# A mixture of 32 experts on one core: both halves of the rows in one stationary, half of w1 multiplied in fp32, and finished rows added into the output by DMA

## What is computed

```python
order = jnp.argsort(flat_e)               # 1024 routed rows, by expert
xb = x_pad[slot_tok].reshape(nb, MOE_BLOCK, D)
hid = jax.nn.silu(xblk @ w1[e]) * (xblk @ w3[e])   # w1, w3: 1024 x 512
yb = hid @ w2[e]                                   # w2: 512 x 1024
y = zeros.at[slot_tok].add(yb * slot_w[:, None])   # weight of the row
x = x + y
```

## Time and profile before

| | before |
|---|---|
| median of 3 runs | 1926.95 us (1926.22 to 1927.83) |
| the profiled execution, its own time | 1926.94 us |
| its span | 1925.1 us |
| TensorE busy | 1723.3 us, 90% |
| VectorE, ScalarE, GpSimd busy | 1145.4, 895.0, 797.3 us |
| bytes moved | 357.94 MB |

### The profile page before, as it was taken

The page is one execution under the profiler, slowest core; times in us unless marked ns, Lnnn a source line. Parts: engine busy times, 40 slices in busy tenths (PEclk is TensorE's granted clock), DMA queues, the critical chain, the costliest instruction groups (busy, mean ns, idle before and its releaser), DMA issues.

```text
span 1925.1 us, 22731 instructions
## 1 busy us (share of the span) xinstructions
PE 1723.3 (90%) x7364; PEld 1250.4 (65%) x7364; DVE 1145.4 (59%) x1523; ACT 895.0 (46%) x1196; POOL 797.3 (41%) x388
## 2 busy tenths in 40 slices
PE   2899999899998989989689997964999999999992
PEld 2788888687785867468577476752666665666661
DVE  5677773725133464334754224225889999999984
ACT  3554443432323220123431034332888888888882
POOL 0688883333341442114101031201566656665562
PEclk9899999999998999989769998976999999999997
DMA  8343443222331434132004322123999999999995
GB/s 284 99 132 110 120 165 125 94 87 73 132 113 65 170 127 161 58 127 88 1 1 129 112 107 88 44 88 104 360 386 397 395 390 390 393 397 394 388 360 186
DMA packets 138669, 357.94 MB, mean 186 GB/s; under 512 B 12661, under 2 KB 64125, under 8 KB 113768
## 3 DMA queue, kind: packets, MB, share of 16 engines
q1 hardware_dynamic: 130050, 324.88, 46.0%
q10 hardware_dynamic: 4758, 19.31, 2.6%
q0 software_dynamic: 3792, 12.85, 2.1%
HBM read 333.95 MB, written 23.07 MB: 185 GB/s over the span
## 4 chain that ended last, share of the span: by engine, by line
PE 54%; issue 17%; POOL 12%; DVE 11%; DMA 2%; ACT 2%; POOLq 0%; DVEq 0%; SPq 0%; ACTq 0%
PE ps L694 13%; PE ps L696 13%; PE ps L695 13%; PE ps L666 10%; POOL parts L2269 9%; PE ps L676 2%; POOL idx L2279 2%; DVE arena L1522 2%; PE ps L899 1%; PE ps L872 1%; DMA arena<-in_x 1%; POOL arena L2282 1%; DVE act_parts L1647 1%; DMA arena<-y_rows,dest_i 1%; DMA ring<-in_w_conv_out 1%
## 5 line engine op out<-in xcount | busy, mean ns | idle before, releaser
L2235 POOL TENSOR_TENSOR parts<-ring,parts 128x1024 fp32r<-128x1024 f32 x150 | 372.9, 2492 | 794.4 <-ACT parts L1058 791.4
L1351 ACT CAST parts<-ring 128x1024 fp32r<-128x1024 f32 x384 | 396.1, 1048 | 90.9 <-PE ps L696 66.9
L694 PE MATMUL ps<-parts,act_parts 128*128 128x512 f32 (+2 forms) x1088 | 427.8, 393 | 7.1 <-DVE parts L2059 2.2
L696 PE MATMUL ps<-parts,act_parts 128*128 128x512 f32 (+2 forms) x1088 | 423.9, 390 | 0.0
L695 PE MATMUL ps<-parts,act_parts 128*128 128x512 f32 (+2 forms) x1088 | 423.8, 390 | 0.0
L2059 DVE TENSOR_TENSOR parts<-ring,parts 128x1024 fp32r<-128x1024 f32 x289 | 394.1, 1415 | 26.4 <-ACT parts L1351 19.8
L2269 POOL TENSOR_TENSOR parts<-ring,parts 128x1024 fp32r<-128x1024 f32 x95 | 264.0, 2779 | 235.7 <-ACT parts L1351 235.0
L1058 ACT CAST parts<-ring 128x1024 fp32r<-128x1024 f32 x150 | 155.6, 1047 | 387.3 <-PE ps L696 297.3
L694 PE MATMUL ps<-act_parts,parts 128*128 128x512 f32 x640 | 253.0, 395 | 10.8 <-DVEq L1649 6.4
L695 PE MATMUL ps<-act_parts,parts 128*128 128x512 f32 x640 | 250.9, 392 | 0.0
L696 PE MATMUL ps<-act_parts,parts 128*128 128x512 f32 x640 | 250.7, 392 | 0.0
(11 more groups left out here) (248 smaller groups left out, 1837.9 us busy)
## 6 DMA issues: line engine op xcount, KB each, us to landing
ring<-in_w SPq DMA_DIRECT2D x192, 1024.0 KB, 7.2
ring<-in_w_in SPq DMA_DIRECT2D x30, 1024.0 KB, 7.2
ring<-in_w_in SPq DMA_DIRECT2D x34, 512.0 KB, 5.1
ring<-in_w_ada SPq DMA_DIRECT2D x12, 1024.0 KB, 14.5
ring<-in_w_ret_out SPq DMA_DIRECT2D x8, 1024.0 KB, 7.3
ring<-in_w_out SPq DMA_DIRECT2D x8, 1024.0 KB, 10.2
y_rows<-arena ACTq DMA_DIRECT2D x32, 256.0 KB, 6.3
ring<-in_w_in SPq DMA_DIRECT2D x16, 256.0 KB, 4.0
```

The lines of the kernel that those rows point to most:

```text
L694: pe.matmul(o, lhs[1], rhs[0], start=start, stop=False)
L696: return pe.matmul(o, lhs[0], rhs[0], start=False, stop=stop)
L1351: act.copy(parts[:, n % 4, 0, :], ring[:, j, n % 4 * 1024:(n % 4 + 1) * 1024]).then_inc(piece_hi, 1)
L2235: pool.tensor_tensor(parts[:, g % 4, 1, :], ring[:, st.place(j), k * 1024:(k + 1) * 1024], parts[:, g % 4, 0, :].bitcast(F32), ALU.subtrac ...
```

## The change

- **One stationary.** High and low rows of x stand side by side (`xgT` is now t, h, n). A piece of w1 or w3 is multiplied with 128 columns by its high half, then by its low half: two matmuls for three. The lower 64 rows of banks 1 and 2 then hold what the low rows gave, which ScalarE copies out (`low_up`) and VectorE adds in (`add_low`), before the sigmoid and the product.
- **w1's first half whole.** Pieces 0 and 1 are not split: four fp32 matmuls read them from the ring, against fp32 rows in `xg_whole` (64 columns of rows, 64 of zeros). Ten pieces a block are left to split (`PER_BLOCK`). The first half of w1 is free when TensorE has used it, and is loaded behind the second.
- **Rows added by DMA.** x is stored to `out` before the loop. The finished rows of a block, weighted already (`slot_w`, a fifth product in routing), are added into `out` by an indirect DMA from GpSimd's queue (`add_to_out`), which each turn waits for at its end (`added`). `y_rows`, its clearing, the store from ScalarE and all after the loop are gone.
- **Empty slots skipped.** An empty slot's index is 2048 or more, and gather and add leave it out (`bounds_check`).

```diff
-    ("h3T", KT, 1), ("route", from_bank(1, 4), 1), ("moe0", (0,), 1), ("moe_first", 4, 1),
+    ("h3T", KT, 1), ("route", from_bank(1, 5), 1), ("moe0", (0,), 1), ("moe_first", 4, 1),
...
+WHOLE = 2
+PER_BLOCK = 12 - WHOLE
...
@@ SyncE
-                for n in range(2):
+                for n in (0, 1) if j else (1, 0):
...
+            sp.dma_start(out_v, x).then_inc(out_done, 16)
...
@@ TensorE, up
-                    o = bank(stage, 1 + j, i)[0:SLOTS, :]
-                    for n in range(4):
+                    o = bank(stage, 1 + j, i)
+                    whole = 0 if j else WHOLE
+                    if whole:
+                        pe.wait_ge(xg_whole_ready, b + 1)
+                        pe.wait_ge(half_landed[0], (b + 1) * 16)
+                    for n in range(whole):
+                        for t in (2 * n, 2 * n + 1):
+                            mm = pe.matmul(o, xg_whole[:, t].rearrange("p h s -> p (h s)"), ring[:, 0, t * 512:(t + 1) * 512],
+                                           start=t == 0, stop=False)
+                        mm.then_inc(piece_split[n], 1)
+                    for n in range(whole, 4):
...
-                            mm = split_product(o, hi_lo(xgT[:, :, t, :]), hi_lo(parts[:, n, :, c * 512:(c + 1) * 512]),
-                                               t == 0, t == KT - 1)
+                            rows = xgT[:, t].rearrange("p h s -> p (h s)")
+                            pe.matmul(o, rows, parts[:, n, 0, c * 512:(c + 1) * 512], start=t == 0, stop=False)
+                            mm = pe.matmul(o, rows, parts[:, n, 1, c * 512:(c + 1) * 512], start=False, stop=t == KT - 1)
...
@@ ScalarE
             def high_rows(stage, k, i=0):
-                act.copy(xgT[:, 0].rearrange("p t n -> p (t n)"), full(stage, k, i)).then_inc(xgT_hi, 1)
+                o = full(stage, k, i).rearrange("p (t n) -> p t n", t=KT)
+                act.copy(xg_whole[:, :, 0, :], o[:, 0:2 * WHOLE, :]).then_inc(xg_whole_ready, 1)
+                act.copy(xgT[:, :, 0, :], o).then_inc(xgT_hi, 1)
...
+            def low_up(stage, j, i=0):
+                act.copy(up_low[j][0:SLOTS, :], full(stage, 1 + j, i)[SLOTS:2 * SLOTS, :]).then_inc(up_low_ready[j], 1)
+            def gate(stage, b, i=0):
+                act.wait_ge(up_sum_ready, b + 1)
+                act.activation(sg_h[0:SLOTS, :], full(stage, 1, i)[0:SLOTS, :], ACT.Sigmoid).then_inc(sg_h_ready, 1)
...
@@ VectorE
-            for n in range(3):
-                low(n, n)
+            low(2, 0)
...
+            own(dve.memset(xg_whole, 0.0))
+            for c in range(2 * MT):
+                own(dve.tensor_scalar(block_w[:, c, :], cst("iota"), blkf[:, c:c + 1], w01[:, c:c + 1], ALU.is_equal, ALU.mult))
...
             def add_rows(c):
-                dve.wait_ge(y_stored, (c + 1) * 16)
+                dve.wait_ge(y_blk_free, c + 1)
...
+            def add_low(stage, j, b, i=0):
+                dve.wait_ge(up_low_ready[j], b + 1)
+                o = full(stage, 1 + j, i)[0:SLOTS, :]
+                moe(dve.tensor_tensor(o, o, up_low[j][0:SLOTS, :], ALU.add))
...
@@ GpSimd
+            def add_to_out(c):
+                pool.wait_ge(y_sum_ready, c + 1)
+                pool.tensor_copy(idx_out[:, :], slot_tok[:, bass.ds(c, 1)]).then_inc(idx_out_ready, 1)
+                pool.wait_ge(idx_out_ready, c + 1)
+                pool.nop().then_inc(settled, 1)
+                pool.indirect_dma_start(out[0], bass.IndirectOffsetOnAxis(ap=idx_out[:, 0:1], axis=0), y_blk[0:SLOTS, :], None,
+                                        bounds_check=S - 1, oob_is_err=False, compute_op=ALU.add).then_inc(y_added, 16)
+            def added(c):
+                pool.wait_ge(y_added, (c + 1) * 16)
+                pool.nop().then_inc(y_blk_free, 1)
...
+            with pool.Fori(0, pool.snap(steps - 1)) as r:
+                turned("moe", r + 1)
+                gather(r + 3)
+                low(3, done + 3 - WHOLE)
+                add_to_out(r)
+                for n in (7, 11):
+                    low(n, done + n - WHOLE)
+                added(r)
```

More of the change, by code:

```diff
@@ L168 @@
 ]
[L169 removed]
+WHOLE = 2
+MOE_PIECES = [("moe_first", [n % 4 for n in range(WHOLE, 8)], 1), ("moe", [n % 4 for n in range(WHOLE, 12)], 1)]
+PER_BLOCK = 12 - WHOLE
 def mix_use(n, k):
@@ L368, in build @@
         taken[0] = expert_free + KT * S
-        combo = carve([4, D])
         y_low = carve([D])
+        up_low = [carve([FF]) for _ in range(2)]
+        xg_whole = carve([2 * WHOLE, 2, SLOTS])
+        block_w = carve([2 * MT, 64])
+        slot_w = carve([64])
         assert taken[0] <= MT * D + 10 * D + 2 * XD + D
@@ L975, in turn_slots @@
                 filled(stage, k, mm)
+            pe.wait_ge(block_w_ready, 1)
+            filled("route", 4, product(bank("route", 4)[0:SLOTS, 0:64], [slot_oh[:, q, :] for q in range(2 * MT)],
+                                       [block_w[:, q, :] for q in range(2 * MT)]))
             pe.wait_ge(plan_ready, 2)
@@ L1354, in _ @@
                 piece_released(act, g)
-            for n in range(4):
+            for n in range(WHOLE, 4):
                 high(n, 0)
@@ L1384, in low_rows @@
                              full("moe", 4 + g, c)[SLOTS:2 * SLOTS, :]).then_inc(y_low_ready, 1)
-            def store_rows(c):
-                act.wait_ge(y_sum_ready, c + 1)
-                act.dma_start(y_rows[bass.ds(c * SLOTS, SLOTS), :], y_blk[0:SLOTS, :]).then_inc(y_stored, 16)
             def down(c):
-                for n in range(3):
-                    high(8 + n, c, used=pieces["moe"].before(8 + n, c))
+                for n in range(8, 11):
+                    high(n, c, used=pieces["moe"].before(n - WHOLE, c))
+                    if n == 8:
+                        gate("moe", c + 1, c)
+                low_up("moe", 1, c)
                 high(11, c, ends=("moe", 2, c))
@@ L2127, in _ @@
             dve.nop().then_inc(plan_ready, 1)
-            own(dve.tensor_copy(slot_tok[:, :], full("route", 3)[0:SLOTS, 0:64]))
+            o = full("route", 3)[0:SLOTS, 0:64]
+            own(dve.tensor_scalar(slot_tok[:, :], o, float(SKIPPED), None, ALU.add))
+            own.wait()
+            own(dve.tensor_scalar(slot_tok[0:1, :], slot_tok[0:1, :], SKIPPED - 1, None, ALU.bitwise_and))
             own.wait()
```

160 lines of the change are left out of this document (76 added, 84 removed).

## The result

The changed kernel takes **1987.63 us** (median of 5 runs, 1978.89 to 1990.63) against 1926.95 of the kernel before: a ratio of 1.031, 95% interval 1.0285 to 1.0333. Slower, where 1896 us was forecast. The profiled run is the shortest of the five. One of the experiments further down, split_all_no_lower, had two disturbed executions of nine, the profiled one among them, so its time is the median of the other seven and it has no turn.

A forecast was written before the change was run, and what follows sets the result against it. Bound: a TensorE, ScalarE and GpSimd ring through one buffer, DMA engines nearly full beside it. Savings 20.7 + 1.8 + 3.9 + 5.1 = 31.5; 1925.1 - 31.5 + 1.8 = 1895.4, said as 1896 us; 8 in 10: 1884 to 1912.

The forecast's parts named there:

- Low 11 meets VectorE at PSUM work alone: 2.45: Loop, chain over GpSimd: its low half of piece 11 takes 2.45 us (2.39 to 2.76), ending at 17.1.
- chain of mine: Loop: two chains, over GpSimd (17.1 us) and over ScalarE (16.9), the longer counting; turn taken as 17.2, 5.1 saved.
- a sigmoid that waits: Loop, chain over ScalarE: the sigmoid also waits for VectorE's sum, up to 0.3 us more.
- The weighing of exclusion: Loop, piece 7's low half: the rule could cost 1.2 us (time 1914); rows show half, so 2.9 us taken.
- The bound is a ring of TensorE, ScalarE and GpSimd: Loop before the change: a closed chain through the one buffer of pieces 3, 7 and 11 sets the 17.37 us turn.
- The end: After the last sum of rows: index copy, one indirect DMA and its landing replace 27.7 us; 20.7 us saved.
- Start and blocks before the loop: Routing: 1.8 us saved; two `up`s outside the loop, each 1.96 us shorter: 3.9 us saved.
- The fp32 matmuls: In each `up`, four fp32 matmuls at 0.89 us each, 3.56 us together.
- The slower rival: Loop: GpSimd waits for the add's landing; from 10.7 us slower than before, at 14.5 the time 2045; chance 0.07.
- The 2.5 us more: Loop, each add: the rule on GpSimd writing descriptors would cost some 2.5 us more; the rows showed nothing of it.
- The ring or the DMA engines come out longer: Rival, loop: index checks, piece 7's low half or two stores cost more; turn 17.6 to 17.9, 1908 to 1917 us; chance 0.20.

The follow-up runs named there:

- split_all_no_lower: Changed kernel with pieces 0 and 1 split again, lower rows neither copied nor added, sigmoid and gate in their old places; 1930.34 us.
- gate_first: Changed kernel with one order changed: VectorE's gate stands ahead of the low half of piece 8; 1917.85 us.
- low11_on_vector: Changed kernel with the low half of piece 11 made by VectorE, GpSimd making only those of pieces 3 and 7; 1926.82 us.
- add_late: Changed kernel with the add issued between GpSimd's low halves of pieces 7 and 11, its landing waited for in the next turn; 1952.64 us.
- gate_first_low11_vector: gate_first with the low half of piece 11 made by VectorE; 1908.90 us.
- five_buffers: Changed kernel with a fifth buffer for split pieces, pieces 4 and 5 split ahead of the rows of the block before; 1998.71 us.

## Why the prediction was wrong, step by step

Cut into parts by the medians: the DMA part -17.9 us, products and lower rows with the gate ahead of low 8 +8.8, the gate behind low 8 +69.8.

- **The step that failed: "Low 11 meets VectorE at PSUM work alone: 2.45".** It came at low 10's start instead, and the price is not on low 11, which takes 2.46, but on low 10, which no chain of mine contained. 30 turns of 19.76 for 17.2 are 77 of the 84 us by which the profiled span is above the forecast one. VectorE came first in four of those 30 turns, and these are shorter (18.2 to 18.4 us from one first fp32 matmul of TensorE to the next, the others 19.1 to 20.9), but not 17.2. With low 10 never held, in gate_first, the turn is 17.64, 0.4 above the forecast. Why the gate matters: low 8 can't start before low 7 ends, whatever is ahead of it, so work on PSUM ahead of low 8 is hidden and behind it comes on top. I had the edit in the text only as a sigmoid that waits, on ScalarE's side. The section on the change doesn't show it either: VectorE's queue was gate, low 8, 9, 10 and became low 8, gate, low 9, 10.
- **The weighing of exclusion went the wrong way.** I set GpSimd's 3.04 us against the Trainium skill's rule in "SBUF — State Buffer", section "Who interferes with whom", took 0.65 for half an exclusion and went by it. The exclusion is whole, and 0.65 is what was left of VectorE's low 6 when low 7 began. The kernel before shows it on the *other* engine, in rows that I hadn't laid beside GpSimd's:
```profile
1507.62 3.50 DVE L2059 TENSOR_TENSOR parts<-ring,parts 128x1024 fp32r<-128x1024 f32 x3 [0.42 <-ACT parts L1351]
1511.03 0.68 DVE L2161 TENSOR_TENSOR arena<-ps,arena 64x512 f32<-64x512 f32 x1
1511.93 4.80 DVE L2059 TENSOR_TENSOR parts<-ring,parts 128x1024 fp32r<-128x1024 f32 x3 [0.22 <-DVE arena L2161]
```
  Low 7 (1510.34 to 1513.38) starts 0.77 us ahead of low 6's end and takes 0.7 longer than alone. Low 8, 9 and 10 take 4.80 us in place of 3.50, for low 8 waits until low 7 is over. With the Trainium skill's rule the traces agree in every overlapping pair of low halves: in all 19 traces, from 1330 us on, VectorE's record, where it ends last, does so by 1.08 to 1.16 us, and GpSimd's by 2.21 or more. They agree with the rule's other half too, that an operation with one SBUF input is not held: in gate_first 114 gates and adds from PSUM lie wholly inside a low half of GpSimd and take 0.67 to 0.68 us.
- **"The bound is a ring of TensorE, ScalarE and GpSimd"** left out that low halves cover 0.98 of the time before: 9 of VectorE at a pitch of 1.14 and 3 of GpSimd at 2.36 make 17.3 of 17.37 us. TensorE is as full, so which of the two binds is not shown. But taking 2 us from TensorE gave nothing: gate_first's turn is 17.64.
- **The end** was right in kind: 19.2 saved, not 20.7. The copy starts 0.4 behind the sum, not 0.1, and from the DMA's start to the end are 7.0 us, not 5.8. Not in the sum at all were the 2.6 us by which the stretch from the last low 11 to the last sum grew.
- **Start and blocks before the loop:** 3.3 saved, not 5.7. There too low 11 takes 3.27 us.
- **The fp32 matmuls** cost less than the 0.89 each that was forecast where the clock is up: in gate_first and low11_on_vector the next product starts 3.13 to 3.14 us behind the first of four in nearly every turn, not 3.56. In the changed kernel's loop it is 3.13 to 4.02, the longer where they begin at the lower clock.
- **The add** lands 7.8 us after its issue (median of 17 between 1450 and 1800), and 5.6% of the 16 engines' time is spent in its queue and the gather's. The slower rival needed 10.7 and didn't happen. GpSimd takes 1.5 us for it where the gather takes 1.0 to 1.4 (in add_late the add takes 2.4). The 2.5 us more that the prediction estimated from the Trainium skill's "SBUF — State Buffer", section "SBUF: two separate sides", were not seen in any turn.
- **"The ring or the DMA engines come out longer"**, 17.6 to 17.9 us, is the turn that gate_first shows: 17.64. I had no rival for a worse order.

**Left open:** why the turn doesn't fall under 17.5 us in gate_first and gate_first_low11_vector, where low halves cover only 0.86 and 0.80. The DMA share is 0.96 there, so the weights aren't far off.

## What to carry to other kernels

Where two engines share something exclusively, look for the price on the one that is held, not on the one that runs: put both engines' rows of a turn side by side, and read how long each instruction takes by its place in the turn, never as a group's mean. Then write the queue of the held engine so that work that isn't excluded stands ahead of the instruction that would wait anyway. In a loop that is balanced to a quarter of a us, first move single instructions before taking a part of a change for bad.

## What the runs showed of the hardware

- Alone, a low half of 128 x 1024 takes GpSimd 2.35 us and VectorE 1.22 (starts 1.14 apart in a row). The one that is held is shown as busy all the while and ends its own work behind the other: VectorE 1.08 us after GpSimd's end, in 3.40 us.
- The first to start by the trace isn't always the first to work: in five_buffers VectorE's record starts 0.40 us ahead of GpSimd's, and yet VectorE waited for the whole of it, and GpSimd took its undisturbed 2.36. There are 20 such pairs in that trace, and in the 17 traces without a fifth buffer none.
- Behind TensorE's wait of 2.13 us in the changed kernel (1516.19) four matmuls started 0.23 to 0.34 us apart, the next 0.43 apart at a granted clock of 0.50. Behind its wait of 1.40 us in the same turn (1509.74), and behind 1.03 in low11_on_vector, the matmuls of the piece kept 0.23 to 0.34.
